# Hybrid attention and HGRN2 layer: an earlier load of tile 2's rows, the sample's halves side by side, meta values as halves

## The reference, cut to what matters

```
p = rms_norm(x, norm_w) @ w_in        # columns: attention q | k | v | gate, HGRN2 q | f | i | gate
# head group A: 8 query heads over 2 key heads, window 128, 16 meta keys always visible
s    = q k^T * 64 ** -0.5             # keys: 16 meta, previous block, own block
prob = softmax(concat([s, sink]))[..., :-1]
att  = prob @ v
# head group B: HGRN2, S_t = diag(f_t) S_{t-1} + k_t v_t^T, o_t = S_t^T silu(q_t)
out  = x + concat([att * silu(g_a), rms_norm(hg) * silu(g_h)]) @ w_out
```

## Time and profile before

| | |
|---|---|
| median of 3 runs | 1179.1 us (1178.9 to 1181.05) |
| time of the profiled execution | 1179.18 us |
| its span, first to last instruction | 1177.4 us |
| PE busy | 1146.4 us, 97% of the span |
| DVE busy | 673.2 us, 57% |
| ACT busy | 430.7 us, 37% |
| POOL busy | 334.5 us, 28% |
| mean granted clock of TensorE | 0.990 of full speed |

### The profile page before, as it was taken

How to read it: one execution, slowest core, us unless ns; L and a number is a source line. 1 busy time by engine, 2 the same in 40 slices (tenths; PEclk the granted TensorE clock), 3 DMA queues, 4 the chain that set the end, 5 groups by cost and what they waited for, 6 DMA issues and landing times.

```text
span 1177.4 us, 25662 instructions
## 1 busy us (share of the span) xinstructions
PE 1146.4 (97%) x9378; PEld 947.8 (80%) x9378; DVE 673.2 (57%) x1751; ACT 430.7 (37%) x1242; POOL 334.5 (28%) x324
## 2 busy tenths in 40 slices
PE   6999999999999999999889999999999999999998
PEld 5787888888887787788767888888888888688887
DVE  6655555555555555557854555655666666655443
ACT  6402222222222222224323555555566565433330
POOL 0003233332322233322421222322232227343231
PEclk9989999999999999999989999999999999999999
DMA  8531111111111111106321611121112124444331
GB/s 279 179 108 56 64 64 62 62 62 62 55 61 62 62 62 62 45 24 246 105 90 39 224 54 45 47 78 53 45 47 81 55 78 158 150 151 144 144 142 72
DMA packets 49391, 108.33 MB, mean 92 GB/s; under 512 B 5088, under 2 KB 17888, under 8 KB 49312
## 3 DMA queue, kind: packets, MB, share of 16 engines
q1 hardware_dynamic: 49328, 107.51, 25.9%
HBM read 70.23 MB, written 38.26 MB: 92 GB/s over the span
## 4 chain that ended last, share of the span: by engine, by line
PE 91%; DVE 4%; issue 1%; ACT 1%; POOL 1%; DMA 1%; SPq 0%; DVEq 0%; ACTq 0%; POOLq 0%
PE h_bank_b L873 5%; PE h_bank_a L873 5%; PE h_bank_b L875 5%; PE h_bank_b L874 5%; PE o_bank L2577 5%; PE h_bank_a L875 5%; PE o_bank L2579 5%; PE h_bank_a L874 5%; PE o_bank L2578 5%; PE h_bank_t L857 3%; PE a_bank_a L1847 3%; PE a_bank_a L1848 3%; PE a_bank_a L1849 3%; PE a_bank_b L1847 3%; PE a_bank_b L1848 3%; PE a_bank_b L1849 3%
## 5 line engine op out<-in xcount | busy, mean ns | idle before, releaser
L336 POOL TENSOR_TENSOR h_lv<-h_lv,h_tt 128x256 f32<-128x256 f32 x96 | 85.5, 891 | 276.1 <-PE h_near_b L899 91.9
L591 DVE TENSOR_TENSOR h_lv<-h_lv,h_tt 128x256 f32<-128x256 f32 x96 | 41.1, 428 | 138.9 <-PE h_near_a L899 67.8
L873 PE MATMUL h_bank_b<-h_w_hi,h_h_hi 128*128 128x512 f32 x256 | 106.5, 416 | 0.1
L873 PE MATMUL h_bank_a<-h_w_hi,h_h_hi 128*128 128x512 f32 x256 | 104.5, 408 | 0.0
L1638 DVE CUSTOM_DVE_ANT_0 a_sm<-a_sc,a_hidden,a_neg_sink 128x272 f32<-128x272 f32 x128 | 59.1, 499 | 74.2 <-PE a_sc L1877 74.1
L875 PE MATMUL h_bank_b<-h_w_hi,h_h_lo 128*128 128x512 f32 x256 | 100.9, 394 | 0.0
L874 PE MATMUL h_bank_b<-h_w_lo,h_h_hi 128*128 128x512 f32 x256 | 100.3, 392 | 0.0
L875 PE MATMUL h_bank_a<-h_w_hi,h_h_lo 128*128 128x512 f32 x256 | 100.2, 391 | 0.0
L874 PE MATMUL h_bank_a<-h_w_lo,h_h_hi 128*128 128x512 f32 x256 | 99.9, 390 | 0.0
L1444 ACT ACTIVATE a_prb<-a_sm,a_neg_m 128x256 f32<-128x256 f32 x128 | 64.2, 502 | 70.7 <-DVE a_neg_m L1638 70.6
L1847 PE MATMUL a_bank_a<-a_w_hi,a_h_hi 128*128 128x512 f32 (+1 forms) x208 | 77.1, 370 | 4.6 <-DMA a_h_lo<-h_split 4.6
(11 more groups left out here) (319 smaller groups left out, 2996.8 us busy)
## 6 DMA issues: line engine op xcount, KB each, us to landing
h_split<-h_h_hi SPq DMA_DIRECT2D x17, 512.0 KB, 3.3
h_split<-h_h_lo SPq DMA_DIRECT2D x17, 512.0 KB, 4.2
a_h_hi<-h_split SPq DMA_DIRECT2D x17, 512.0 KB, 3.4
a_h_lo<-h_split SPq DMA_DIRECT2D x17, 512.0 KB, 4.3
h_x<-x_prompt SPq DMA_DIRECT2D x16, 512.0 KB, 3.5
o_m<-mixed SPq DMA_DIRECT2D x16, 512.0 KB, 4.5
o_x<-x_prompt SPq DMA_DIRECT2D x16, 512.0 KB, 4.3
y_prompt<-o_x SPq DMA_DIRECT2D x16, 512.0 KB, 2.6
```

The lines of the kernel that those rows point to most:

```text
L336: ins = pool.tensor_tensor(new[:, :, 0, :], old[:, :, 0, :], right.unsqueeze(2).to_broadcast([P, HW // (2 * b), b]), ALU.mult)
L873: pe.matmul(out[:, :], h_hi[t.slot][:, k, :], hi, start=(k == 0), stop=False)
```

## The change

1. `load_h(tile(0, 2))` moves ahead of the spreading of the meta values, to the end of the part of SP's order before it, and there ahead of a store of HGRN2's.
2. The meta probabilities are written twice side by side (`PM` has a copy axis), so two transposes in place of one give 2 x 128 rows; ACT rounds them to F32R, DVE subtracts to leave low halves in rows 64 to 127 (`meta_low`), and PE multiplies by high and by low halves of the meta values, four products of 256 columns. 24 small DMAs spread the halves, where there were 8, and POOL clears two buffers of 512 columns, where there was one.
3. `k_nat` and the small statistics move into the memory that `QS` also uses. So the stores of `new_win_k` and `new_win_v` move up in SP's order, behind the load of blocks 2 and 3 of `w_out`, and `q_split` of the last tile waits for them. `o_norm` writes `MIX` directly.
4. The sample's high and low halves stand side by side in one buffer `s_rows` of 40 columns per chunk, so that 2 products per chunk give both (32 in all); POOL clears the buffer once the last `mix` is done, and DVE adds two rows of results instead of one.
5. In DVE's order of the output stage `s_lo` moves ahead of the first three `add_x`, and `split_sums(2, 1)` from before the last `o_norm` to behind `sum_4`.

Smaller edits: semaphores are merged, counts adjusted, ACT copies `PTS` before `PMT`.

```diff
@@ attention, buffers @@
+        k_nat = squares("k_nat", [P, KVH * HD])
         QS = sb("qs", [P, AH, 2, HD], F32R)
-        VMD = sb("vmd", [P, HW])
+        VMH = sb("vmh", [P, KVH, HW // 2], F32R)
+        VML = sb("vml", [P, KVH, HW // 2], F32R)
@@ attention, sync @@
             sp.dma_start(new_meta_v, v_nat_0[0:META, :]).then_inc(meta_stored, 16)
+            load_h(tile(0, 2))
             yield
-            sp.wait_ge(v_placed, 1)
+            sp.wait_ge(v_meta_split, 2)
             sp.wait_ge(buffers_zeroed, 2)
             for h in range(AH):
...
+                for copy in range(2):
+                    sp.dma_start(VMH[at:at + META, kv, c].bitcast(F32), v_meta_hi[:, source].bitcast(F32)).then_inc(v_meta_spread, 16)
+                    if copy == 0:
+                        sp.dma_start(VML[at:at + META, kv, c].bitcast(F32), v_meta_lo[:, source].bitcast(F32)).then_inc(v_meta_spread, 16)
-            load_h(tile(0, 2))
...
             sp.wait_ge(kv_proj, TILES)
             yield
-            store_mixed(tile(0, TILES - 2))
-            yield
             sp.wait_ge(k_normed, TILES)
             sp.wait_ge(v_copied, TILES)
             sp.dma_start(new_win_k, k_nat[:, :]).then_inc(rest_stored, 16)
             sp.dma_start(new_win_v, v_nat[:, :]).then_inc(rest_stored, 16)
+            store_mixed(tile(0, TILES - 2))
+            yield
             store_mixed(tile(0, TILES - 1))
@@ attention, vector @@
             def q_split(t):
                 dve.wait_ge(q_done, t.n + 1)
+                if isinstance(t.n, int) and t.n == TILES - 1:
+                    dve.wait_ge(rest_stored, 4 * 16)
                 dve.tensor_copy(QS[:, :, 0, :], heads(q_nat[:, :])).then_inc(q_high, 1)
...
+            def meta_low(t):
+                dve.wait_ge(pm_split, 2 * t.n - 1)
+                dve.tensor_tensor(PMT[64:P, :, :], pt[64:P, :, 2 * P:3 * P], PMT[64:P, :, :].bitcast(F32), ALU.subtract).then_inc(pm_split, 1)
...
                     denominators(last)
+                    meta_low(last)
                 gate_plus(t0)
@@ attention, tensor @@
-                    ins = pe.transpose(pt[:, 0, 2 * P:3 * P], PM[:, :, :].rearrange("p h k -> p (h k)"), ident[:, :])
+                    for kv in range(KVH):
+                        ins = pe.transpose(pt[:, kv, 2 * P:3 * P], PM[:, kv, :, :, :].rearrange("p c g k -> p (c g k)"), ident[:, :])
...
-                    pe.matmul(bank_o[:, :], PMT[:, :], VMD[:, :], start=False, stop=True).then_inc(o_ready, 1)
+                    pe.wait_ge(pm_split, 2 * t.n)
+                    for kv in range(KVH):
+                        out = bank_o[:, kv * HW // 2:(kv + 1) * HW // 2]
+                        pe.matmul(out, PMT[:, kv, :], VMH[:, kv, :], start=False, stop=False)
+                        ins = pe.matmul(out, PMT[:, kv, :], VML[:, kv, :], start=False, stop=(kv == 1))
+                    ins.then_inc(o_ready, 1)
@@ output, gpsimd @@
+            pool.wait_ge(attention["mix_done"], TILES)
+            pool.memset(s_rows[:, :, :].bitcast(F32), 0.0).then_inc(sums_made, 1)
@@ output, vector @@
             def add_sample(a):
                 dve.tensor_tensor(X_S[:, cols(a)], bank_s[a][0:NS, :], X_S[:, cols(a)], ALU.add).then_inc(y_added, 1)
+                dve.wait_ge(y_added, 5 + 2 * a)
+                dve.tensor_tensor(X_S[:, cols(a)], bank_s[a][SROW:SROW + NS, :], X_S[:, cols(a)], ALU.add).then_inc(y_added, 1)
...
             split_sums(1, 0)
-            split_sums(2, 1)
             yield
...
-            add_x(tile(0, 0), 0)
-            add_x(tile(0, 0), 1)
             dve.wait_ge(high, 5)
-            dve.tensor_tensor(flat(s_lo), bank_t[0][:, 0:KT * NS], flat(s_hi).bitcast(F32), ALU.subtract).then_inc(low, 1)
-            add_x(tile(0, 1), 0)
+            dve.tensor_tensor(s_lo, bank_t[0][:, 0:KT * NS].rearrange("p (k t) -> p k t", t=NS), s_hi.bitcast(F32), ALU.subtract).then_inc(low, 1)
+            for i in range(2):
+                for a in range(2 - i):
+                    add_x(tile(0, i), a)
...
             sum_4(n)
+            split_sums(2, 1)
             add_x(tile(0, 1), 1)
@@ output, tensor @@
             def multiply_sample(a, first, end):
                 pe.wait_ge(low, 5)
+                for k in range(first, end):
+                    rows = s_rows[:, k, :]
+                    pe.matmul(bank_s[a][0:SROW + NS, :], rows, w_hi[a][:, k, :], start=(k == 0), stop=False)
+                    ins = pe.matmul(bank_s[a][0:SROW + NS, :], rows, w_lo[a][:, k, :], start=False, stop=(k == KT - 1))
```

More of the change, by code:

```diff
@@ L1445, in exps @@
                                    accum_out=row_sum[:, h:h + 1])
-                    ins = act.activation(PM[:, h, :], SM[j % 2][:, i, 0:META], ACT.Exp, bias=neg_m[:, h:h + 1], scale=-1.0,
+                    meta = SM[j % 2][:, i, 0:META].unsqueeze(1).to_broadcast([P, 2, META])
+                    ins = act.activation(PM[:, h // 4, :, h % 4, :], meta, ACT.Exp, bias=neg_m[:, h:h + 1], scale=-1.0,
                                          accum_out=row_sum_meta[:, h:h + 1])
@@ L1453, in place_p @@
                 wait(act, pv_done, 4 * (t.n - 1) + j)
+                act.activation(PTS[:, :, :], pt[:, :, 0:2 * P], ACT.Copy).then_inc(p_placed, 1)
                 if j == 3:
-                    act.activation(PMT[:, :], pt[:, 0, 2 * P:3 * P], ACT.Copy)
-                act.activation(PTS[:, :, :], pt[:, :, 0:2 * P], ACT.Copy).then_inc(p_placed, 1)
+                    act.activation(PMT[:, :, :], pt[:, :, 2 * P:3 * P], ACT.Copy).then_inc(pm_split, 1)
             def sink_exp(t):
@@ L1817, in vector @@
             denominators(t0)
+            meta_low(t0)
             gate_plus(end)
@@ L1834, in vector @@
             denominators(end)
+            meta_low(end)
             yield
@@ L2362, in scalar @@
             act.wait_ge(turned, 5)
-            act.wait_ge(attention["mix_done"], TILES)
             act.wait_ge(attention["rest_stored"], 4 * 16)
-            act.activation(flat(s_hi), bank_t[0][:, 0:KT * NS], ACT.Copy).then_inc(high, 1)
+            act.wait_ge(sums_made, 4 * HK + 1)
+            act.activation(s_hi, bank_t[0][:, 0:KT * NS].rearrange("p (k t) -> p k t", t=NS), ACT.Copy).then_inc(high, 1)
             def copy_p1(p):
@@ L2589, in multiply_sample @@
                 pe.wait_ge(low, 5)
-                return products(bank_s[a][0:NS, :], lambda k: s_hi[:, k, :], lambda k: s_lo[:, k, :],
-                                lambda k: w_hi[a][:, k, :], lambda k: w_lo[a][:, k, :], range(first, end), first == 0, end == KT)
+                for k in range(first, end):
+                    rows = s_rows[:, k, :]
+                    pe.matmul(bank_s[a][0:SROW + NS, :], rows, w_hi[a][:, k, :], start=(k == 0), stop=False)
+                    ins = pe.matmul(bank_s[a][0:SROW + NS, :], rows, w_lo[a][:, k, :], start=False, stop=(k == KT - 1))
+                return ins
             t0, t1 = tile(0, 0), tile(0, 1)
```

65 lines of the change are left out of this document (34 added, 31 removed).

## The result

The changed kernel takes 1185.2 us (median of 8 runs, 1181.9 to 1186.9), the kernel before 1179.0: a ratio of 1.005, interval 1.0038 to 1.0061. It is slower by 6.2 us, and outside the predicted range, by 1.2 us. Its profiled execution took 1186.03, span 1184.2, 6.8 more than before.

The account below looks back on a forecast made before the run. PE was taken as the bound, 80.00 of 80 us busy in the attention loop. Gains of 3.4, 5.2 and 2.1 less a loss of 10.7 summed to 0.0: 1179.2 us, range 1173 to 1184.

Parts of the forecast that it names:

- D: Start of output: fewer sample products and moved splits gain 2.1 us (0.5 to 5.6), with PE waiting 3 us for DVE.
- A: Wait at 606: loading tile 2's rows earlier removes PE's 4.61 us wait, gaining 3.4 us (2.5 to 3.7).
- C: Last tile of attention: tile 16's query cast waits for two stores behind `w_out` blocks, losing 10.7 us, 2.2 of it clock.
- B: Attention loop: four F32R meta products replace one, saving 0.35 us per tile over 15 tiles, a gain of 5.2 us.
- The rival by which the stores don't stand behind the blocks: Last tile of attention: stores overtake the blocks, PE loses 4.5 us in place of 10.7; 1173.0 us, chance 0.15.
- the lower bound in the text: Attention loop: meta products save only 0.24 us per tile, 3.6 in all, if entering and leaving the F32R run costs a tenth.
- one sign by which the prediction called itself wrong: Attention loop: the prediction is wrong if a tile is not some 0.35 us shorter.
- the third, the clock: TensorE's clock stays low longer behind the waits of A, C and D, adding 3.5 us: 1182.7 us, chance 0.25.

Follow-up runs that it names:

- filled: Changed kernel plus PE products with unused results in both waits (before tile 16's first `turn_q` and the first pair's third `turn_block`): 1180.5 us.
- stores_first: Changed kernel with the stores of `new_win_k` and `new_win_v` issued ahead of the output stage's loads: 1175.5 us.
- old_sample: `stores_first` with the sample's halves again as two operands (48 products) and the second block's splits again ahead of the last `o_norm`: 1175.7 us.
- rows_early: Kernel before with only the load of tile 2's rows moved ahead of the spreading DMAs: 1175.7 us.
- values_spread: Changed kernel with stores ahead of output loads, sample additions and block 3's splits later, sample's value products spread between tile 2's query projection products: 1169.5 us.
- all_moved: `order_proj` with the sample's short value products also spread between tile 2's query projection products: 1166.0 us.
- order_proj: Changed kernel: sample additions, block 3's splits later; stores between mixed-row loads and `w_out` blocks; tile 2's second key/value projection half before sample's scores: 1167.4 us.

## Why the prediction was wrong

The waits of the sum are right: each that it named is there, released by what it named. What it left out is the clock behind D's wait, and the other terms failed in size, in this trace all to the same side.

**D is the step that failed**: "Gain 2.1", with "From there PE is the bound again" and no term for the clock behind a wait of 3 us. It missed by more than any other term, 2.9. PE got 5.51 ahead, as the 5.6 of the sum. Then it waited 3.90 for `operand(ahead, 0)` where 3 stood, and the wait was followed by 5.60 us for transposes and block 3 where before had 3.19: -5.51 + 3.90 + 2.41 = 0.80 lost. Of the 0.9 by which the wait was longer, 0.3 is rounding (the sum's own 1035.4 less 1032.1 is 3.3). The rest is DVE's chain, which grew by 4.35 where the sum had 3.6 (it also began 0.2 earlier than the sum had): before, it ran 11.61 us from this line to the end of `operand(ahead, 0)` at 1035.51,

```profile
1023.90 0.69 DVE L2478 TENSOR_TENSOR o_a_lo<-o_bank,o_a_hi 128x512 fp32r<-128x512 f32 x1 [2.52 <-ACT o_a_hi L2373]
```

and in the changed kernel 15.96, from 1026.07 to 1042.03. The four additions are 0.3 of that, 2.75 from the first to the next operand at 1037.63 where the sum had 1.27 + 1.2:

```profile
1026.07 0.69 DVE L2511 TENSOR_TENSOR o_a_lo<-o_bank,o_a_hi 128x512 fp32r<-128x512 f32 x1 [1.61 <-ACT o_a_hi L2405]
...
1034.88 0.67 DVE L2495 TENSOR_TENSOR o_x_s<-o_bank,o_x_s 8x512 f32<-8x512 f32 x1
...
1037.63 0.67 DVE L2511 TENSOR_TENSOR o_a_lo<-o_c,o_a_hi 128x512 fp32r<-128x512 f32 x1
1038.23 2.48 DVE L2483 TENSOR_TENSOR o_t_lo<-o_t_raw,o_t_hi 128x512 fp32r<-128x512 f32 x4
1040.64 0.67 DVE L2511 TENSOR_TENSOR o_a_lo<-o_s,o_a_hi 128x512 fp32r<-128x512 f32 x1
1041.34 0.69 DVE L2511 TENSOR_TENSOR o_a_lo<-o_bank,o_a_hi 128x512 fp32r<-128x512 f32 x1
```

The larger fault is the clock: A and C had a term for it, D had none, though a wait of 3 us was forecast and the earlier trace rows show 0.64 behind one of 1.6 us. Counted from tile 16's meta product, block 3 starts 1.2 earlier than before (the sum had 2.1), and from its start to the fourth `turn_block` it takes 4.86 us in place of 2.84: 2.0 lost behind the point at which the sum stopped. `filled` shows that the 2.4 is the clock: with PE busy in the wait it shrinks to 3.44 - 3.19 = 0.25.

**C**: 11.42 in the table and 11.7 by `stores_first`, forecast 10.7 (10.35 with tile 15's share of B taken off, as the table has it). The wait was 9.15 (forecast 8.5), and the 2.5 beside it are the clock (forecast 2.2; `filled` gives 2.7). The queue in the changed kernel:

```profile
962.01 10.88 SPq L2242 DMA_DIRECT2D o_t_raw<-w_out  x4
972.99 0.45 SPq L1312 DMA_DIRECT2D new_win_k<-a_k_nat  x1
973.48 0.65 SPq L1313 DMA_DIRECT2D new_win_v<-a_v_nat  x1
```

and DVE's cast behind it:

```profile
980.74 0.43 DVE L1623 CAST a_qs<-a_q_nat 128x512 fp32r<-128x512 f32 x1 [9.18 <-DMA new_win_v<-a_v_nat]
```

The last store was out by 974.1 and the cast could start at 980.74, 6.6 later; 32 KB on an idle queue took 1.8. The packets of the transfers in the trace show that it is the order and not a shared rate. The two stores are 256 packets of 512 bytes. From 974.1, when both are issued, to 978.8, 916 packets with 1.84 MB start, at 392 GB/s, and not one of them is of that size; from 978.8 to 980.3, as the last of the blocks goes, all 256 start. The rival by which the stores don't stand behind the blocks is refuted.

**B**: forecast 0.35 per tile, measured 0.24 over the loop. The row of four was priced at 0.12 each; it takes 0.56 from its first start to the transposes behind it, since the first one, which comes after products of 64 columns, has 0.20 to the next start:

```profile
788.15 0.36 PE L1931 MATMUL a_bank_o<-a_vmh,a_pmt 128*128 128x256 f32 x1
788.35 0.28 PE L1932 MATMUL a_bank_o<-a_vml,a_pmt 128*128 128x256 f32 x1
...
788.71 0.60 PE L1886 MATMUL a_bank_t<-c_ident,a_qs 128*128 128x128 f32 x4
```

0.91 - 0.56 - 0.11 for the second transpose = 0.24, which was the lower bound in the text. So one sign by which the prediction called itself wrong came in: a tile is not some 0.35 shorter. 3.33 us in the loop in place of 14 x 0.35 = 4.9. DVE's subtraction was hidden: the one wait for it in the whole kernel is 0.21.

**A**: 3.5 alone by the medians, forecast 3.4, so the term was right by them, though not the clock in it; 1.65 in the trace of the changed kernel: the wait is shorter (2.10 in place of 4.61), and a low clock came at 624 to 632. Within the spread of that stretch (48.15 to 51.44 for `filled`, `stores_first` and `old_sample`, which have the same code there) both numbers are possible.

**The rival that came nearest** is the third, the clock: 1182.7, at 0.25. It named the places and put 3.5 on them, and was still 2.5 below the measured time. The filling got 4.9 of clock back in C and D together (2.7 and 2.2), where the sum had 2.2. Against the forecast the trace missed 1.7 in A (3.4 to 1.65), 1.6 in B's loop (4.9 to 3.33), 1.1 in C (10.35 to 11.42) and 2.9 in D (2.1 gained to 0.8 lost), less 0.4 at the start: 6.9, for the 6.8 of the spans. The range ended at 1184 because its cases were taken one by one; B near its bound, C's longer wait and the clock behind D came together.

The page TensorE: Matmul & The Clock Gate of the Trainium skill (section Part 1: The HAM clock gate) says that an idle TensorE falls to 1.2 GHz and comes back only after sustained work. `filled` agrees with it: behind both waits the clock is 1.00 in place of 0.50.

The page DMA: Bandwidth & Descriptors of the Trainium skill (section Queues, rings and completion order) says that each DMA engine takes its descriptors in ring order. The stores agree with it: 6.6 us from their issue to the cast, with all of their packets behind 978.8.

## What to carry to other kernels

The waits of 9.15 and 3.9 us here were paid twice: their length, and what the low clock took behind them, 1.3 to 2.7 us by execution. Shorter waits had a low clock behind them too (0.74 behind 2.26 us in `old_sample`, 0.64 behind 1.6 us); leave no new wait of PE without a second term. Where an edit lets one buffer lie over another, look at what stands ahead of the store that empties it: two stores of 64 KB behind two blocks of 1 MB cost 11.7 us, and ahead of all the loads 1.0. Work put on the engine that becomes the next to end last (here DVE's splits and additions) takes the gain of a shorter PE row; ask for its place behind what PE is waiting for.

## What had not been expected of the hardware

The clock fell with PE 4.00 of 4 busy, in and behind the row of the sample's short value products (0.50 at 624 to 628 in the changed kernel), and did not when products of 512 columns stood between them (1.00 in `values_spread` and in `all_moved`, where `order_proj` has 0.56 and 0.59 from 620 to 628). So a stretch that reads as full in the busy time can still lose the clock.

The start differs from run to run with the same code: PE's clock in 50 to 100 us is 0.90 in `before` and `filled`, 0.93 in most of the others, 0.97 in `after`, `rows_early` and `order_proj`, and the same product starts at:

```profile
94.48 0.46 PE L899 MATMUL h_near_a<-h_lv,h_kz 128*32 128x32 f32 x32 [0.88 <-DVE h_lv L584]
```

in `before`, and at

```profile
91.76 0.46 PE L899 MATMUL h_near_a<-h_lv,h_kz 128*32 128x32 f32 x32 [0.85 <-DVE h_lv L584]
```

in `after`. A chance of 2.7 us in one execution is larger than the sum's term for D (2.1) and not far below that for A (3.4). It need not last, either: at the first landmark `after` is only 0.40 ahead.
